# A decoder step on one core: key rows at 4.5 units a pair, a fifth of their sums on ScalarE, new places for low parts and gathers, and two lists joined through PSUM

## The reference, cut to what matters

```python
h = rmsnorm(x, norm_mix_g)
q, k, v, qi, ki, wi, cx, cb, cc, ga, gb = split(h @ w_in)      # 2048 -> 11344 columns
# sample tokens: an indexer scores the 2052 positions, the best 256 of each token are kept
score = einsum(relu(qi . ki) , wi);  idx = top_k(score, 256)
ks, vs = cache_k[page(idx)], cache_v[page(idx)]                # 8 heads x 128 floats a row
logits = einsum(q, ks) * 128**-0.5 + rel_bias[bucket(q_pos - idx)]
attn   = softmax(logits) @ vs
# prompt tokens: the same with the best 64 positions, as masks over 256 x 256
x += (sigmoid(ga) * (attn @ w_pa) + sigmoid(gb) * ((cb * conv(cc * cx)) @ w_pb)) @ w_o
x += square(relu(rmsnorm(x, norm_mlp_g) @ w_mlp_in)) @ w_mlp_out;  y = rmsnorm(x, norm_final_g)
```

## Time and profile before

| | |
|---|---|
| median of 3 runs | 1877.49 us (1876.36 to 1881.3) |
| the profiled execution | 1884.36 us, its span 1882.6 us, mean granted clock 0.977 |
| PE, DVE, ACT, POOL busy | 95%, 57%, 37%, 28% of the span |
| pairs 15 to 29 (key rows) | 314.9 to 589.9 us |
| pairs 30 to 37 (value rows) | 589.9 to 747.7 us |

### The profile page before, as it was taken

The page is one execution under the profiler, slowest core; times in us unless marked ns, Lnnn a source line. Parts: engine busy times, 40 slices in busy tenths (PEclk is TensorE's granted clock), DMA queues, the critical chain, the costliest instruction groups (busy, mean ns, idle before and its releaser), DMA issues.

```text
span 1882.6 us, 32492 instructions
## 1 busy us (share of the span) xinstructions
PE 1790.6 (95%) x13691; PEld 1719.5 (91%) x13691; DVE 1078.4 (57%) x1180; ACT 688.8 (37%) x847; POOL 533.0 (28%) x422
## 2 busy tenths in 40 slices
PE   8979997997889999999999999999999999999996
PEld 6946997987778889999999999999999999999996
DVE  5135998799897944435554654444543554455444
ACT  4443443343334445543333432333322333333321
POOL 2812777566665665410023000000000000000131
PEclk8989999999989999999999999999999999999997
DMA  5712555787776898464544444544544545445441
GB/s 219 263 41 68 159 158 168 232 320 269 268 254 214 310 329 284 146 217 160 174 159 160 169 162 159 174 159 160 175 157 162 173 156 166 169 157 168 167 158 71
DMA packets 74787, 349.92 MB, mean 186 GB/s; under 512 B 9903, under 2 KB 12151, under 8 KB 53657
## 3 DMA queue, kind: packets, MB, share of 16 engines
q1 hardware_dynamic: 50496, 270.43, 43.2%
q0 software_dynamic: 19584, 71.31, 10.8%
q10 hardware_dynamic: 4600, 6.67, 1.0%
HBM read 339.45 MB, written 8.80 MB: 185 GB/s over the span
## 4 chain that ended last, share of the span: by engine, by line
PE 82%; DVE 11%; POOL 2%; issue 1%; ACT 1%; DMA 1%; POOLq 0%; ACTq 0%; DVEq 0%
PE PM L428 18%; PE PM L430 18%; PE PM L429 18%; PE PM L408 8%; PE PM L410 7%; PE PM L409 7%; DVE VL L1343 2%; DVE lg L1349 2%; DVE kv L1348 2%; POOL VL L1597 1%; PE PM L393 1%; PE PM L580 1%; PE PM L749 1%; POOL kv L1607 1%; PE PM L589 1%
## 5 line engine op out<-in xcount | busy, mean ns | idle before, releaser
L1488 DVE TENSOR_TENSOR WL<-wring,WH 128x2048 fp32r<-128x2048 f32 x159 | 364.3, 2291 | 341.0 <-ACT WH L828 340.9
L828 ACT ACTIVATE WH<-wring 128x2048 fp32r<-128x2048 f32 (+1 forms) x163 | 307.3, 1885 | 682.4 <-PE PM L430 678.6
L408 PE MATMUL PM<-hH,VH 128*128 128x288 f32 x1408 | 432.1, 307 | 56.4 <-POOL VL L1597 37.9
L409 PE MATMUL PM<-hL,VH 128*128 128x288 f32 x1408 | 421.1, 299 | 0.0
L410 PE MATMUL PM<-hH,VL 128*128 128x288 f32 x1408 | 419.3, 298 | 0.0
L1597 POOL TENSOR_TENSOR VL<-wring,VH 128x512 fp32r<-128x512 f32 x251 | 328.7, 1315 | 236.1 <-ACT VH L828 234.3
L428 PE MATMUL PM<-XH,WH 128*128 128x288 f32 x1280 | 379.2, 296 | 1.5 <-DVE WL L1495 1.5
L428 PE MATMUL PM<-YH,WH 128*128 128x288 f32 x1280 | 379.0, 296 | 0.0
L429 PE MATMUL PM<-YL,WH 128*128 128x288 f32 x1280 | 377.8, 295 | 0.0
L429 PE MATMUL PM<-XL,WH 128*128 128x288 f32 x1280 | 377.8, 295 | 0.0
L430 PE MATMUL PM<-XH,WL 128*128 128x288 f32 x1280 | 376.5, 294 | 0.0
(11 more groups left out here) (258 smaller groups left out, 1670.1 us busy)
## 6 DMA issues: line engine op xcount, KB each, us to landing
wring<-w_in SPq DMA_DIRECT2D x176, 512.0 KB, 4.3
wring<-w_mlp_in SPq DMA_DIRECT2D x64, 1024.0 KB, 5.2
wring<-w_mlp_out SPq DMA_DIRECT2D x64, 1024.0 KB, 5.2
wring<-w_o SPq DMA_DIRECT2D x16, 1024.0 KB, 5.1
wring<-w_pb SPq DMA_DIRECT2D x8, 1024.0 KB, 5.0
wring<-w_pa SPq DMA_DIRECT2D x8, 1024.0 KB
x_store<-zB SPq DMA_DIRECT2D x1, 2304.0 KB, 8.0
xT<-x_store SPq DMA_DIRECT2D x1, 2304.0 KB, 11.3
```

The costliest lines, as they stand in the source:

```text
L408: pe.matmul(out, vh, hH[:, k, :], start=(k == 0), stop=False)
L409: pe.matmul(out, vh, hL[:, k, :], start=False, stop=False)
L828: return act.activation(out, in_, ACT.Copy, **kw)
L1488: dve.tensor_tensor(WL[:, i % 2], wring[:, i % 2], WH[:, i % 2], ALU.subtract).then_inc(S["wl_ready"], 1)
```

## The change

1. Key units are placed at 4.5 a pair: unit n's place is eighth `unit_end(n)`, from pair 15 to eighth 1 of pair 29.
2. Of the key units 3, 8, ..., 58 (12 of them) VectorE only multiplies; ScalarE sums the eight heads by eight copies in place with an accumulated output, four before and four after one high part.
3. VectorE has no low parts in pair 15, eighths 2 and 6 of pairs 16 to 29, the odd ones of pairs 30 to 37, and none from pair 38 on.
4. GpSimd issues gathers at places given by `unit_end`, the first five with one low part between each two. A gather waits for `unit_added` where ScalarE reads the slot.
5. The joining of the two lists keeps one operand of every step in PSUM. The spread of `comb` moves behind the first eighth of pair 14.
6. Two of the eight `prompt_top` rounds move ahead of the spread; the `rbk` tables move behind the row numbers; the steps of the softmax in pair 29 move to eighths 3, 4 and 7.

```diff
+NEWKEY = 35
+ACT_UNITS = [n for n in range(UNITS - 4) if n % 5 == 3]
+def unit_end(n):
+    return 8 * KP + (3 + 32 * n // 9) // 2
 def dve_low(u):
     p, j = divmod(u, 8)
-    return j % 2 == 1 if p >= VP else p >= KP and j in (2, 5, 7)
+    return KP < p < VP and j in (2, 6) or VP <= p < VP + 8 and j % 2 == 1
...
-            pairs(9, KP)
-            pe.wait_ge(S["comb_ready"], 1)
...
+            pairs(9, KP - 1)
+            def picked(j):
+                if j == 0:
+                    pe.wait_ge(S["comb_ready"], 1)
...
+                    m.then_inc(S["spread_done"], 1)
+            win_half(KP - 1, 0, picked)
+            win_half(KP - 1, 1)
...
             def tops(j):
-                if j == 1:
+                if j == 3:
                     pe.wait_ge(S["ul_copied"], 2)
                     pe.wait_ge(S["tmax_ready"], 1)
                     transpose(bank(4, 0, P, H), small[:, 0:H]).then_inc(S["tmax_turned"], 1)
-                elif j == 3:
+            def sums(j):
+                if j == 0:
                     pe.wait_ge(S["tmax_wide"], 1)
                     transpose(bank(7, 0, H), smx).then_inc(S["tmax_back"], 1)
-            def sums(j):
-                if j == 2:
+                elif j == 3:
                     pe.wait_ge(S["lsum_ready"], 1)
...
+            def unit_sums(at):                                   # ScalarE
+                for i, n in enumerate(ACT_UNITS):
+                    if unit_end(n) + 1 == at:
+                        highs(at + 4)
+                        act.wait_ge(S["prod_ready"], i + 1)
+                        for h in range(H):
+                            if h == H // 2:
+                                highs(at + 5)
+                            k_ = kv[:, n % RK, h * HD:h * HD + HD]
+                            m = copy(k_, k_, accum_out=lg[:, n, h:h + 1])
+                        m.then_inc(S["unit_added"], 1)
...
-            highs(UNIT * (VP - 1) + 8)
+            highs(UNIT * (VP - 1) + 9)
...
-            gt, same, first = (scw[0:NS, TOPK * i:TOPK * i + TOPK] for i in range(3))
+            dve.wait_ge(S["qn_copied"], 2)
+            bval, bpos, same, apart = (bank(5 - i // 2, TOPK * (i % 2), TOPK, NS) for i in range(4))
+            gt, first = scw[0:NS, 0:TOPK], scw[0:NS, TOPK:2 * TOPK]
...
+            dve.tensor_tensor(apart, apos, bpos, ALU.subtract)
             step(dve.tensor_tensor(same, same, first, ALU.mult))
             step(dve.tensor_tensor(gt, gt, same, ALU.add))
-            step(dve.tensor_tensor(first, apos, bpos, ALU.subtract))
-            step(dve.tensor_tensor(first, first, gt, ALU.mult))
+            step(dve.tensor_tensor(first, apart, gt, ALU.mult))
...
+            for i in range(2):
+                prompt_top(i)
...
-            def weigh(rows, out):
+            def weigh(rows, out, by_act=False):
                 by2 = rows.rearrange("p (a b) -> p a b", a=2)
-                step(dve.tensor_tensor(by2, by2, PM[:, 6:8, :], ALU.mult))
-                return dve.tensor_reduce(out, rows.rearrange("p (h d) -> p h d", h=H), AX_X, ALU.add)
+                m = dve.tensor_tensor(by2, by2, PM[:, 6:8, :], ALU.mult)
+                if by_act:
+                    m.then_inc(S["prod_ready"], 1)
+                else:
+                    step(m)
+                    dve.tensor_reduce(out, rows.rearrange("p (h d) -> p h d", h=H), AX_X, ALU.add).then_inc(S["unit_read"], 1)
...
-                weigh(kv[:, n % RK, :], lg[:, n, :]).then_inc(S["unit_read"], 1)
-                lows(UNIT * KP + 7 + 8 * (n + 1) // 5)
+                weigh(kv[:, n % RK, :], lg[:, n, :], n in ACT_UNITS)
+                lows(unit_end(n) + 3)
...
                 if RK <= n < UNITS + RK:                          # GpSimd, gather(n)
-                    pool.wait_ge(S["unit_read"], n - RK + 1)
+                    k, added = n - RK, sum(m <= n - RK for m in ACT_UNITS)
+                    if k in ACT_UNITS:
+                        pool.wait_ge(S["unit_added"], added)
+                    else:
+                        pool.wait_ge(S["unit_read"], k + 1 - added + (k > NEWKEY))
...
-            lows(UNIT * KP + 4)
+            lows(UNIT * KP)
             pool.wait_ge(S["rows_ready"], 1)
...
             for n in range(UNITS + RK):
+                lows(UNIT * KP + n if n < RK else unit_end(n - RK) + 4)
                 gather(n)
-                lows(UNIT * KP + 4 + max(0, 8 * (n - 3) // 5))
```

More of the change, by code:

```diff
@@ L988, in oneb_copy @@
                 copy(onebT[:, 512 * g:512 * g + 512], bank(4 + g % 2)).then_inc(S["oneb_copied"], 1)
+            def unit_sums(at):
[9 more added lines that the diff above has]
+                        m.then_inc(S["unit_added"], 1)
             for p in range(12, 16):
                 if p == KP:
+                    for c in range(4):
+                        unit_sums(UNIT * p + c)
                     highs(UNIT * p + 8)
@@ L994, in _ @@
                     oneb_copy(1)
+                    for c in range(4, 8):
+                        unit_sums(UNIT * p + c)
                     highs(UNIT * p + 12)
@@ L998, in _ @@
                 evac(p, vT[:, 2 * (p - 12):2 * (p - 12) + 2, :])
+            for c in range(4):
+                unit_sums(UNIT * 16 + c)
             highs(UNIT * 16 + 8)
@@ L1028, in _ @@
             for p in range(16, 28):
-                for c in (1, 3, 5, 7):
+                for c in range(4 if p == 16 else 0, UNIT):
+                    unit_sums(UNIT * p + c)
                     n = 4 * (p - KP - 1) + c // 2 - 2
-                    if 0 <= n < 17:
+                    if c % 2 and 0 <= n < 17:
                         highs(UNIT * p + c + 5)
@@ L1065, in gate @@
                 evac(p, g[:, 2 * (p % 36 % 28):2 * (p % 36 % 28) + 2, :], ACT.Sigmoid)
+            for c in range(UNIT):
+                unit_sums(UNIT * 28 + c)
             act.wait_ge(S["up_ready"], 1)
             gate(28)
-            highs(UNIT * (VP - 1) + 8)
+            highs(UNIT * (VP - 1) + 9)
             act.wait_ge(S["lg_shifted"], 1)
@@ L1331, in _ @@
             step(dve.tensor_reduce(comb[:, UNITS, :], eqn, AX_X, ALU.max))
+            step(dve.memset(rbs[0:1, :], 0.0))
+            dve.wait_ge(S["rb_in"], 16)
+            step(dve.memset(rbk[:], 0.0))
+            step(dve.tensor_tensor(rbs[:], rb[:], rbs[:], ALU.subtract))
+            for i in range(4):
+                dve.tensor_copy(rbk[NB * i:NB * i + NB, H * i:H * i + H], rbs[:]).then_inc(S["rbk_ready"], 1)
             dve.tensor_tensor(oneb, dist[:].unsqueeze(2).to_broadcast([P, UNITS, NB]),
@@ L1359, in _ @@
                     dve.tensor_scalar(newsel[:], bank(4, 0, 1), -1.0, -OFF, ALU.add, ALU.mult).then_inc(S["newpos_read"], 1)
-                elif n == 35:
+                elif n == NEWKEY:
                     dve.wait_ge(S["nat_copied"], 14)
-                    step(weigh(knrep[:], qstep_k[:]))
+                    weigh(knrep[:], qstep_k[:])
+                    dve.wait_ge(S["unit_read"], n + 2 - sum(m <= n for m in ACT_UNITS))
                     dve.wait_ge(S["newpos_read"], 1)
@@ L1384, in _ @@
             past = lg[:, 0:UNITS, :]
-            dve.wait_ge(S["unit_read"], UNITS)
+            dve.wait_ge(S["unit_read"], UNITS + 1 - len(ACT_UNITS))
+            dve.wait_ge(S["unit_added"], len(ACT_UNITS))
             dve.wait_ge(S["bias_copied"], 1)
@@ L1396, in _ @@
             dve.tensor_tensor(lg[:], lg[:], bank(7, 0, H).unsqueeze(1).to_broadcast([P, UNITS + 1, H]), ALU.subtract).then_inc(S["lg_shifted"], 1)
-            lows(UNIT * (VP - 1) + 8)
+            lows(UNIT * (VP - 1) + 9)
             dve.wait_ge(S["lg_exp"], 1)
@@ L1411, in spread_unit @@
                 spread((1 + v) % 2, lg[:, v, :].unsqueeze(2).to_broadcast([P, H, NS]))
-            def prompt_top(i):
-                for a, b in ((0, P), (P, 3 * P)):
-                    step(dve.max(m8p[:], mask2[:, a:b]))
-                    step(dve.match_replace(mask2[:, a:b], m8p[:], mask2[:, a:b], MARK))
             def prompt_row(h):
@@ L1462, in _ @@
                     if p == VP:
-                        prompt_top(c)
+                        if c < TOPP // 8 - 2:
+                            prompt_top(c + 2)
                         if c == UNIT - 1:
```

22 lines of the change are left out of this document (9 added, 13 removed).

## The result

The kernel after takes 1854.62 us (median of 4 runs, 1853.32 to 1860.61), the kernel before 1878.69 beside it (4 runs). The ratio is 0.9878, 95% interval 0.9852 to 0.9904. The profiled execution after took 1860.61 us.

A forecast was written before the change was run, and what follows sets the result against it. PE, 95% busy, was taken to be held by late low parts because VectorE is full from pair 17. Savings 12.1 + 5.4 + 26 - 0.5 - 2.4 = 40.6 us; 1877.5 - 40.6 = 1837 us, range 1820 to 1858.

The forecast's parts named there:

- Join and spread: Joining the lists before pair 15: 3.8 us instead of 10.9, row numbers 8.3 us, first gather 8.2 us earlier.
- Pair 15: First pair with key units: 18.0 us against 30.1, saving 12.1, since VectorE's chain no longer precedes a low part.
- Pairs 17 to 20: Key pairs with VectorE's load down to 12.3 us a pair: 63.0 us against 68.4, saving 5.4; ends 61 and 67.
- ScalarE's sums: Pairs 21 to 28: GpSimd waits 1.0 us at each of seven units that ScalarE sums, 7 us in all.
- Pairs 21 to 28: Later key pairs: 117 us against 143.0, saving 26; ends 104 and 134.
- base: Pairs 21 to 28: GpSimd's low parts and gathers become the bound at 13.2 us a pair, 105.6 in all.
- unit 35: Key unit carrying 4.2 us more VectorE work for the new tokens: about 2.5 us of stall.
- unit 49 and the turns: Unit 49 has 3.5 us more before a low part, costing 1 us; turns in pair 26 cost 0.9.
- rival on long sums: ScalarE's sums take 0.59 us a head, GpSimd waits 3 us instead of 1, 24 less saved: 1861 us; chance 0.13.
- Transfers: Pairs 21 to 28: weights land later at 305 GB/s, 0.3 us a pair added, 2.4 us lost.
- VectorE is full: 15.8 us a pair, more than PE's 12.8: From pair 17 on, five key units and three low parts a pair overload VectorE, making low parts late.
- rival of a closing ring: ScalarE waits for VectorE's product; each of 12 units holds PE up to 5.8 us, at worst 1895 us; chance 0.05.

The follow-up runs named there:

- e3: Kernel after with the ten steps joining the two lists back in SBUF, the spread staying behind the first eighth of pair 14: 1863.94 us.
- e2: Kernel after with all 64 key units summed by VectorE and none by ScalarE: 1840.60 us.
- e4: Kernel after with one more GpSimd low part ahead of each of the twelve gathers into a slot that ScalarE reads: 1845.44 us.
- e5: e2 with the five small steps on the new tokens' logits moved from key unit 35 to one each behind units 36 to 40: 1835.84 us.
- e12: e2 with VectorE's low parts behind each key unit four eighths further on, as in the kernel before (3 becomes 7): 1877.46 us.
- e1: Kernel after with VectorE's read of the new positions' mask (`newsel`) moved from key unit 4 to unit 6: 1855.72 us.
- e8: Kernel before with only the join through PSUM, the moved spread, the two picking rounds ahead of it and bias tables behind the row numbers: 1875.12 us.
- e9: Kernel before with VectorE's low parts behind each key unit made only up to four eighths nearer (7 becomes 3): 1863.08 us.
- e6: e2 with key units placed at 5 a pair instead of 4.5, and `newsel` at unit 6: 1846.42 us.
- e10: e2 with the new tokens' small steps spread out, VectorE's third low part back, and the convolution's input split over units 44 to 49: 1833.46 us.
- e7: e2 with VectorE making the low parts of eighths 2, 5 and 7, as before the change, instead of 2 and 6: 1838.92 us.

## Why the forecast was right in its direction and 17.6 us too low

- *Join and spread.* Right. Steps of 0.40 to 0.42 against 0.4 priced, and e3 confirms that the place of the operands is their cause. `comb` was ready at 296.9, not 299.5, because the start is earlier too. The row numbers took 7.2 us from the spread's end for 8.3 priced: not three but two steps grew by 1.0 (one with two SBUF inputs, one a conversion). The offsets came 2.2 us before the 312.0 forecast.
- *Pair 15: 18.0 forecast, 19.4 taken*, with waits of 2.9 us instead of 12.4 and a clock of 0.91. "No idle time above 2 us" fails: one gather of the five took 2.83 us instead of 0.95 (below), the low part behind it was late, TensorE waited 2.4 us, and eighths 122 and 123 took 4.28 and 4.04.
- *Pair 16: nothing forecast, 1.6 us lost.* TensorE is busy all through it before and after; the granted clock is 0.84 for 0.91. In e2 it is 0.91 again, and 19.9 us.
- *Pairs 17 to 20: 63.0 forecast, 67.7 taken.* The step that failed is the one left out: I charged ScalarE's sums to pairs 21 to 28 alone, with seven units, though the rivals count twelve. Without them it is 61.3 (e2), the lower end. Three of the 6.4 us between are in pair 18 (see transfers).
- *Pairs 21 to 28: 117 forecast, 128.2 taken.* The forecast's terms against e2 and the kernel after:
```
                        forecast   measured
base                    105.6      102.4   (8 x 12.80, reached in five pairs of e2)
ScalarE's sums          7          9.9     (128.2 after, 118.3 e2)
unit 35                 2.5        7.9     (pair 23 of e2, over 12.80)
unit 49 and the turns   1 + 0.9    8.0     (pairs 26 and 27 of e2, over 12.80)
```
  *The base.* "It becomes the bound: 8 x 13.2" is not what ran: pairs 21 and 22 of e2 take 12.80 us each with the same GpSimd work. The price itself was near: from 415 to 437 us GpSimd has no idle time above 0.16 us there, so it had been ahead by enough for two pairs. The pairs with stalls, 23, 26 and 27, let it catch up. Whether it would bind over eight pairs without a stall no run shows.
  *The sums.* "It waits 1.0" was 2.8. The rival on long sums had priced 3 (1861), close to the wait and wrong in its mechanism: the read of the accumulator does overlap. TensorE lost 1.4 us a unit here for 1.0 forecast; over all stages 14 us for twelve units against the 7 us counted. e4 shows where it came from: with one low part ahead of that gather 9.2 of the 14 us go.
  *Units 35 and 49*, the largest misses. Their steps were priced from the kernel before (4.2 and 3.5 us; its trace has 3.8 and 3.5), where GpSimd stood idle beside the small ones. In the kernel after GpSimd makes low parts beside them, and the same blocks take 7.9 us (450.36 to 458.22) and 8.1 (503.42 to 511.54). Timelines of DVE and POOL before:
```profile
463.14 0.75 DVE L1366 SCALAR_TENSOR_TENSOR lg<-rbr,cp,lg 128x8 f32<-128x8 f32 x3
515.24 0.91 DVE L1376 TENSOR_TENSOR uv<-zB,G 128x32 f32<-128x32 f32 x8
516.18 0.17 DVE L1380 COPY sp<-uv 128x16 f32<-128x16 f32 x1
```
```profile
466.87 0.95 POOL L1607 DMA_INDIRECT kv<-cache_k,offs  x1 [4.36 <-DVE lg L1349]
519.14 1.15 POOL L1607 DMA_INDIRECT kv<-cache_k,offs  x1 [6.70 <-DVE lg L1349]
```
  Timelines of DVE and PE after (the 3.59 us of unit 35 are shown at e5):
```profile
505.74 2.67 DVE L1420 TENSOR_TENSOR uv<-zB,G 128x32 f32<-128x32 f32 x8
508.44 3.05 DVE L1424 COPY sp<-uv 128x16 f32<-128x16 f32 x1
```
```profile
511.67 1.04 PE L398 MATMUL PM<-cp,sp 128*18 128x128 f32 x8 [1.94 <-DVE sp L1425]
```
  So the gain itself made these blocks longer: GpSimd no longer waits, and its low parts run beside VectorE's small steps. In e12, where GpSimd again waits 6.7 us, the eight steps take 0.90 us and the copy 0.18; in e2, where it doesn't, the eight steps take 4.90. Behind unit 35 VectorE's low part of eighth 186 is 5.11 us late, and that eighth then takes 3.05 us for 1.6.
  Of what was to show, the wait for VectorE's sums below 15 came true (10.5), and GpSimd above 85% busy did not: 98.95 of 128.2 us, 77%.
- *Pair 29: 14.0 forecast, 16.3 taken*, inside the ends given. A step of 128x512 with both inputs in SBUF took 3.31 us.
- *Transfers: 2.4 us lost.* In pairs 21 to 28 not seen: pair 22 of e2 runs at 12.80 us at 349 GB/s, with the DMA engines busy to 0.96. In pair 18 of the kernel after they did hold it. From 372 to 376 us the DMA engines are busy throughout (share 1.03 and 1.04) at 422 and 424 GB/s, a high part waits 2.6 us for its weights and a key unit 1.2 for its rows, and eighth 147 takes 4.96 us for 1.95 in e2. e1 and e3 have a wait of 2.4 and 3.2 us at the same place, e2 has none and e4, which keeps ScalarE's sums, 0.9; what brings the transfers together there, no run shows. Windows of e2, and timeline of ACT after:
```profile
423.80:436.60 12.80, 12.80 (x98) 12.80 (x97) 12.12 (x12) 5.60 (x9) 12.00 (x11) 1.00 0.96 349
```
```profile
375.49 0.63 ACT L837 ACTIVATE VH<-wring 128x512 fp32r<-128x512 f32 x1 [2.64 <-DMA wring<-w_in]
```
- *The cause of the stalls before.* "VectorE is full: 15.8 us a pair, more than PE's 12.8" was the reason that the forecast gave for the gain, and it comes second. The waits for sums of the earlier trace rows were there because VectorE stood ahead of them in a wait for a high part (its 30.9 us for ACT VH stand in the same group, and I did not use that row). Pairs 21 to 28 by the two differences:
```
                             5 units a pair            4.5 units a pair
low parts early (+7)         143.0 before, 141.6 e8    145.3 e12
low parts late (+3)          133.1 e9, 127.6 e6        118.3 e2
```
Three steps of this table change one thing that matters (e6 also has `newsel` at 6, which made no difference in e1): before to e9 (10 us by the order at five units), e12 to e2 (27 by the order at 4.5) and e6 to e2 (9 by the lesser load in the new order). In the old order less load seems to bring nothing (141.6 to 145.3), but e12 has VectorE's third low part on GpSimd too, so that step is not clean. The order is worth 16 us by itself (e9); without it the new arrangement less ScalarE's sums is worth about 3 (e12). The line that the prediction doesn't mention, `lows(unit_end(n) + 3)`, is thus the first of the edits. That the forecast had the direction right is in part luck: it argued from the load, and an edit that it left out carried the gain. The rival of a closing ring named a loop of the same engines, closed at ScalarE's wait for a product, and gave it 0.05 as something that the change might cause; a loop of this kind, closed at VectorE's wait for a high part, was what the kernel before already had.

What stays open: why VectorE falls behind in pairs 25 to 27 of e5 and e10 (14.4 to 18.8 us each), where e7, with more low parts on VectorE, takes 12.80, 17.28 and 13.28; and whether ScalarE's sums pay if they are placed earlier than the gather needs them.

## What to carry to other kernels

When two engines feed a third through a short ring and each also has work that the other waits for, look at who stands idle *ahead* of the work that is called late: an engine at 88% busy can be the cause by its order, not its load. Put work that is ready before a step that waits for the pace setter. In a list kept in order, price a new wait by what stands behind it, for every place where it occurs. Don't take the length of a small step from a stretch in which the engine that it collides with stood idle. And try the one-digit shift of an order before moving work between engines.

## What the runs showed of the hardware

A gather's issue on GpSimd mostly takes 0.95 to 1.4 us (the timeline rows above), but two of the 64 in the kernel after took 2.83 and 2.31. Each ran beside a VectorE step of 128x2048 with two SBUF inputs: one of 3.94 us from 315.70 on, one of 2.28 us from 503.42 on. Timeline of POOL:
```profile
317.65 2.83 POOL L1651 DMA_INDIRECT kv<-cache_k,offs  x1 [0.16 <-issue]
504.22 2.31 POOL L1651 DMA_INDIRECT kv<-cache_k,offs  x1 [1.28 <-ACT kv L837]
```
The row of 3.59 us at key unit 35 is three steps of 8 elements a partition: two of them took 0.23 and 0.29 us, the third 3.0, more than a weigh of 1024. GpSimd had two low parts running beside it (455.46, 2.49 us). Eight copies of 128x128 with accumulated output run 0.29 us apart, their reads of 0.19 hidden. The Trainium skill (VectorE: DVE Perf Modes, "The TRN2 errata") gives 350 cycles of 1.2 GHz for such a copy from SBUF, which is 0.29 us, and the trace agrees: 296 ns on the mean of 96.
